# Merging heads while the last pair is divided, sparse scores three steps ahead, and part of the compressed branch on GpSimd

## What is computed

```
for l in range(DEPTH):
    h = modulate(rms_norm(x, norm1_g[l]), sh1, sc1)
    qa, ka, va, qb, kb, vb, ga, gb = split_in_proj(h @ w_in[l])
    ya = window_attention_latent(rope(qa), rope(ka), va, kac, vac, sink_a[l])
    yb = full_attention_latent(rope(qb), rope(kb), vb, kbc, vbc)
    x = x + gt1 * ((sigmoid(ga) * (ya @ w_pa) + sigmoid(gb) * (yb @ w_pb)) @ w_o)
    x = x + gt2 * swiglu(modulate(rms_norm(x, norm2_g[l]), sh2, sc2), ...)
```

```
s = q @ kc + bias;  p_cmp = masked_softmax(s, dist >= 0);  o_cmp = p_cmp @ vc
s = q @ kb + bias;  o_slc = masked_softmax(s, causal) @ vb
s = q @ kw + bias;  o_win = masked_softmax(s, causal) @ vw
y_a = (sum of sigmoid(br_gate) * (o_cmp, o_slc, o_win)) * silu(g_nsa) @ w_proj_a
```

## Time and profile before

| | |
|---|---|
| timed runs, us | 2504.87, 2505.83, 2508.88 (median 2505.83) |
| profiled execution | 2507.7 us, its span 2505.8 us |
| TensorE busy | 2395.6 us, 96%, 13215 matmuls |
| VectorE busy | 1570.5 us, 63%, 2476 instructions |
| ScalarE busy | 1121.6 us, 45%, 1776 instructions |
| GpSimd busy | 146.1 us, 6%, 261 instructions |
| mean granted clock of TensorE | 0.985 of 2.4 GHz |
| weight splits on VectorE (L185) | 288 of 1.22 us |
| mean DMA rate | 107 GB/s |

### The profile page before, as it was taken

The page is one execution under the profiler, slowest core; times in us unless marked ns, Lnnn a source line. Parts: engine busy times, 40 slices in busy tenths (PEclk is TensorE's granted clock), DMA queues, the critical chain, the costliest instruction groups (busy, mean ns, idle before and its releaser), DMA issues.

```text
span 2505.8 us, 34512 instructions
## 1 busy us (share of the span) xinstructions
PE 2395.6 (96%) x13215; PEld 2047.7 (82%) x13215; DVE 1570.5 (63%) x2476; ACT 1121.6 (45%) x1776; POOL 146.1 (6%) x261
## 2 busy tenths in 40 slices
PE   7999999899999999999999998999999999888898
PEld 3888878788888888888778876899999978777677
DVE  4776777788666554454676776644443565487764
ACT  4647777723321121122647775332222355565541
POOL 0200000110000000000100001000000010000010
PEclk8999999999999999999999999999999999999999
DMA  6421111353333333322221113422222333421153
GB/s 278 145 72 45 52 38 45 120 227 125 145 134 118 125 128 135 118 76 84 101 76 52 51 51 128 141 85 95 91 95 91 110 114 139 143 80 61 69 200 110
DMA packets 67961, 268.88 MB, mean 107 GB/s; under 512 B 8432, under 2 KB 8496, under 8 KB 66528
## 3 DMA queue, kind: packets, MB, share of 16 engines
q1 hardware_dynamic: 42336, 162.94, 18.4%
q0 software_dynamic: 25472, 103.82, 11.6%
HBM read 238.42 MB, written 27.26 MB: 106 GB/s over the span
## 4 chain that ended last, share of the span: by engine, by line
PE 80%; DVE 6%; issue 6%; ACT 5%; DMA 2%; POOL 0%; SPq 0%; ACTq 0%; DVEq 0%; POOLq 0%
PE ps L189 22%; PE ps L191 22%; PE ps L190 22%; PE ps L1199 1%; PE ps L1200 1%; PE ps L1201 1%; PE ps L1133 1%; PE ps L1140 1%; DMA ada_raw<-in_ada 1%; DVE inv L1385 1%; PE ps L1182 1%; ACT pr L1263 1%; PE ps L813 1%; DVE maxes L1358 1%; PE ps L1217 1%
## 5 line engine op out<-in xcount | busy, mean ns | idle before, releaser
L189 PE MATMUL ps<-h_hi,w_hi 128*128 128x512 f32 (+2 forms) x2680 | 920.8, 344 | 28.8 <-DVE h_lo L1479 15.1
L191 PE MATMUL ps<-h_hi,w_lo 128*128 128x512 f32 (+2 forms) x2680 | 907.1, 338 | 0.0
L190 PE MATMUL ps<-h_lo,w_hi 128*128 128x512 f32 (+2 forms) x2680 | 906.6, 338 | 0.0
L189 PEld LDWEIGHTS ps<-h_hi,w_hi 128*128 128x128 f32 x2680 | 509.5, 190 | 91.4 <-issue 29.6
L191 PEld LDWEIGHTS ps<-h_hi,w_lo 128*128 128x128 f32 x2680 | 509.1, 190 | 56.9
L190 PEld LDWEIGHTS ps<-h_lo,w_hi 128*128 128x128 f32 x2680 | 508.8, 190 | 55.7 <-issue 2.4
L185 DVE TENSOR_TENSOR w_lo<-w_raw,w_hi 128x1024 fp32r<-128x1024 f32 x288 | 351.9, 1223 | 166.5 <-ACT w_hi L178 166.3
L178 ACT ACTIVATE w_hi<-w_raw 128x1024 fp32r<-128x1024 f32 x288 | 302.6, 1052 | 306.5 <-PE ps L191 292.0
L191 PE MATMUL ps<-q_hi,w_lo 128*128 128x512 f32 x720 | 256.8, 357 | 0.0
L190 PE MATMUL ps<-q_lo,w_hi 128*128 128x512 f32 x720 | 256.5, 356 | 0.0
L189 PE MATMUL ps<-q_hi,w_hi 128*128 128x512 f32 x720 | 256.1, 356 | 0.0
(11 more groups left out here) (358 smaller groups left out, 3058.7 us busy)
## 6 DMA issues: line engine op xcount, KB each, us to landing
w_raw<-in_stream SPq DMA_DIRECT2D x288, 512.0 KB, 3.5
wt<-in_ada_t POOLq DMA_DIRECT2D x72, 512.0 KB, 3.8
ada_raw<-in_ada SPq DMA_DIRECT2D x4, 2048.0 KB, 19.1
x_keep<-x POOLq DMA_DIRECT2D x8, 768.0 KB, 7.1
gates<-th_g POOLq DMA_DIRECT2D x16, 384.0 KB, 2.6
x<-x_keep POOLq DMA_DIRECT2D x2, 3072.0 KB, 12.3
gates<-sg POOLq DMA_DIRECT2D x24, 256.0 KB, 2.3
wt_q<-in_ada_t POOLq DMA_DIRECT2D x8, 512.0 KB, 3.8
```

Of the source, the lines that this page charges most:

```text
L189: nc.tensor.matmul(out_ap, lh, rh, start=start, stop=False)
L190: nc.tensor.matmul(out_ap, lh, rl, start=False, stop=False)
L191: return nc.tensor.matmul(out_ap, ll, rh, start=False, stop=stop)
```

## The change

Four things are changed.

- TensorE's wait for the memsets (`ready.base + 4`) moves from step -8 to `turn(0)`, which is the first to read `maxes` (`spread` is read later, by `sink`).
- `h_hi` of the first pairs (two in layer 0, three in layer 1) is copied by ScalarE inside the attention's last steps (`pair_high`). VectorE's steps end at T; the last pair's `divide` moves into the merge, piece by piece between the first `h_lo`s. TensorE does the first four chunks of unit 0 and of unit 1 in turn, then the rest of 0, then the rest of 1. The wait for `y_taken` comes ahead of unit 1's second half, and the one for `taken` ahead of all.
- In the sparse attention three gate chunks stand ahead of the first scores instead of one, `scores` run three steps ahead and behind the turn (they were two ahead and in front of it), gate chunks three ahead (one before). ScalarE's `gate` is at step 5 of a head (it was step 0 of the next). VectorE's `cmp_shift` is at step 0 (was 1), its weight split at step 4 (was 1), and `cmp_scale` is cut in two: `cmp_sum` stays on VectorE at step 3, and the product with the branch gate and the last product run on GpSimd, as does `prep` from head 2 on. GpSimd has its own order (`pool_own`).
- The semaphores of "nsa", "lru" and "cmp" are taken from the one shared set "second".

```diff
+            y_high, = signals("heads", y_high=CH)
+            early_pair = {T - 1: 0, T + 1: 1} if both else {T - 1: 0, T: 1, T + 1: 2}
...
                     if n == 0:
+                        e.wait_ge(ready.sem, ready.base + 4)
...
                     for q in now:
                         gate_chunk(q)
-                    if t == -PRO:
-                        e.wait_ge(ready.sem, ready.base + 4)
...
+                    if t in early_pair:
+                        if t == T - 1:
+                            e.wait_ge(unit_done, 1 + base + N_GATE)
+                        pair_high(e, early_pair[t])
+            def pair_high(e, c):
+                e.wait_ge(divided.sem, divided.base + parts * (c + 1))
+                nc.scalar.activation(h_hi[:, c, 0:wide], qf[:, c, 0:wide], ACT.Copy).then_inc(y_high.sem, 1)
+            def divide(e, u, piece):
...
-                for t in range(-PRO, T + LAG + 10):
+                for t in range(-PRO, T):
...
-                    for u in range(NU):
+                    for u in range(NU - parts):
                         n = parts * (2 * (u // parts) + 1) + u % parts
                         since = t - (final[n] + LAG + 3 + 2 * (u % parts))
                         if 0 <= since < pieces[n]:
-                            divide(u, since)
...
+                def chunk(n, c):
+                    at, s, cols = 2048 * (n % 2) + 1024 * (c // 4), (base + n) % 3, slice(c * P, c * P + P)
                     if n == 0:
-                        e.wait_ge(done["gated"].sem, done["gated"].base + N_GATE)
-                        e.wait_ge(done["maxed"].sem, done["maxed"].base + done["tiles"])
-                    elif n == 1:
-                        e.wait_ge(done["taken"].sem, done["taken"].base + done["ring"])
-                        e.wait_ge(done["y_taken"].sem, done["y_taken"].base + done["outputs"])
-                    else:
-                        e.wait_ge(gated.sem, gated.base + n - 1)
+                        e.wait_ge(y_low.sem, y_low.base + c + 1)
+                    for s0, size in groups:
+                        mm = three(psf[:, at + s0:at + s0 + size], w_hi[:, s, cols], w_lo[:, s, cols],
+                                   h_hi[:, c, s0:s0 + size], h_lo[:, c, s0:s0 + size], c % 4 == 0, c % 4 == 3)
+                    return mm
+                e.wait_ge(lo_ready, base + 2)
+                e.wait_ge(done["gated"].sem, done["gated"].base + N_GATE)
+                e.wait_ge(done["maxed"].sem, done["maxed"].base + done["tiles"])
+                e.wait_ge(done["taken"].sem, done["taken"].base + done["ring"])
+                for c in range(4):
+                    chunk(0, c)
+                    chunk(1, c)
+                for c in range(4, 8):
+                    mm = chunk(0, c)
+                mm.then_inc(unit_done, 1)
+                e.wait_ge(done["y_taken"].sem, done["y_taken"].base + done["outputs"])
+                for c in range(4, 8):
+                    mm = chunk(1, c)
+                mm.then_inc(unit_done, 1)
+                for n in range(2, CH):
+                    e.wait_ge(lo_ready, base + n + 1)
+                    e.wait_ge(gated.sem, gated.base + n - 1)
                     for c in range(CH):
-                        if n == 0:
-                            e.wait_ge(y_low.sem, y_low.base + c + 1)
-                        at, s, cols = 2048 * (n % 2) + 1024 * (c // 4), u % 3, slice(c * P, c * P + P)
-                        for s0, size in groups:
-                            mm = three(psf[:, at + s0:at + s0 + size], w_hi[:, s, cols], w_lo[:, s, cols],
-                                       h_hi[:, c, s0:s0 + size], h_lo[:, c, s0:s0 + size], c % 4 == 0, c % 4 == 3)
+                        mm = chunk(n, c)
                     mm.then_inc(unit_done, 1)
             def act(e):
-                e.wait_ge(unit_done, 1 + base)
-                for c in range(CH):
-                    e.wait_ge(done["divided"].sem, done["divided"].base + parts * (c + 1))
-                    nc.scalar.activation(h_hi[:, c, 0:w], qf[:, c, 0:w], ACT.Copy).then_inc(y_high.sem, 1)
+                for c in range(done["pairs_high"], CH):
+                    done["pair_high"](e, c)
...
+                last = parts * (CH - 1)
                 for c in range(CH):
                     e.wait_ge(y_high.sem, y_high.base + c + 1)
                     nc.vector.tensor_tensor(h_lo[:, c, 0:w], qf[:, c, 0:w], h_hi[:, c, 0:w].bitcast(F32), ALU.subtract).then_inc(y_low.sem, 1)
+                    if c < 2:
+                        done["divide"](e, last, 2 * c)
+                        done["divide"](e, last, 2 * c + 1)
+                    if c == 2 and parts == 2:
+                        done["divide"](e, last + 1, 0)
+                        done["divide"](e, last + 1, 1)
...
-                gate_chunk(0)
+                for q in range(3):
+                    gate_chunk(q)
                 e.wait_ge(cmp["biased"].sem, cmp["biased"].base + 2)
                 e.wait_ge(cmp["gated"].sem, cmp["gated"].base + 12)
                 scores(0)
                 scores(1)
+                scores(2)
                 for n in range(M):
-                    if n + 2 < M:
-                        scores(n + 2)
                     if n % 8 == 0:
                         cmp_scores(n // 8)
                     turn(n)
+                    if n + 3 < M:
+                        scores(n + 3)
                     if n % 8 == 4:
                         cmp_turn(n // 8)
                     if n % 4 == 1 and n >= 4:
                         values(n // 4 - 1)
-                    if n + 1 < M:
-                        gate_chunk(n + 1)
+                    if n + 3 < M:
+                        gate_chunk(n + 3)
...
-                    if n % 8 == 0 and n:
-                        gate(n // 8 - 1)
+                    if n % 8 == 5:
+                        gate(n // 8)
...
-                def cmp_scale(hd):
-                    pair, g = hd // 2, hd % 2
-                    at = 4 * g + pair
+                def cmp_sum(hd):
                     e.wait_ge(c_exp.sem, c_exp.base + hd + 1)
                     dve_own.link(e, nc.vector.tensor_reduce(cmp_n[:, 1, :], cmp_s[:, :, :], AX_X, ALU.add))
-                    dve_own.link(e, nc.vector.reciprocal(cmp_n[:, 2, :], cmp_n[:, 1, :]))
-                    dve_own.link(e, nc.vector.tensor_tensor(cmp_n[:, 3, :], br_cols[:, :, at:at + 1].rearrange("p r a -> p (r a)"),
-                                                            cmp_n[:, 2, :], ALU.mult))
-                    dve_own.link(e, nc.vector.scalar_tensor_tensor(cmp_s[:, :, :], bias_of(hd), -NEG / 2, cmp_s[:, :, :],
-                                                                   ALU.is_lt, ALU.mult))
-                    nc.vector.tensor_tensor(cmp_s[:, :, :], cmp_s[:, :, :], bc(cmp_n[:, 3, :]), ALU.mult).then_inc(c_scaled.sem, 1)
+                    nc.vector.reciprocal(cmp_n[:, 2, :], cmp_n[:, 1, :])
+                    nc.vector.scalar_tensor_tensor(cmp_s[:, :, :], bias_of(hd), -NEG / 2, cmp_s[:, :, :], ALU.is_lt,
+                                                   ALU.mult).then_inc(c_summed.sem, 1)
...
-                    if n % 8 == 1:
+                    if n % 8 == 0:
+                        cmp_shift(hd)
+                    if n % 8 == 4:
                         split_lo(e, base + hd + 2)
-                        cmp_shift(hd)
-                    if n % 8 == 2 and 1 <= hd and hd + 1 < H:
-                        prep(hd + 1)
                     if n % 8 == 3:
-                        cmp_scale(hd)
+                        cmp_sum(hd)
...
+                def prep(hd):
+                    pair, g = hd // 2, hd % 2
+                    e.wait_ge(a_ready.sem, a_ready.base + 2 * hd + 1)
+                    nc.gpsimd.tensor_tensor(qb[half[g], hd % 2, :], qf2[half[g], pair, :], qa[half[g], hd % 2, :].bitcast(F32),
+                                            ALU.subtract).then_inc(b_ready.sem, 1)
+                    e.wait_ge(b_ready.sem, b_ready.base + hd + 1)
+                def cmp_scale(hd):
+                    pair, g = hd // 2, hd % 2
+                    at = 4 * g + pair
+                    e.wait_ge(c_summed.sem, c_summed.base + hd + 1)
+                    pool_own.link(e, nc.gpsimd.tensor_tensor(cmp_n[:, 3, :], br_cols[:, :, at:at + 1].rearrange("p r a -> p (r a)"),
+                                                             cmp_n[:, 2, :], ALU.mult))
+                    nc.gpsimd.tensor_tensor(cmp_s[:, :, :], cmp_s[:, :, :], bc(cmp_n[:, 3, :]), ALU.mult).then_inc(c_scaled.sem, 1)
+                    e.wait_ge(c_scaled.sem, c_scaled.base + hd + 1)
                 e.wait_ge(cmp["spilled"].sem, cmp["spilled"].base + 64)
                 for hd in range(2):
                     e.dma_start(bias[:, hd, :], bias_in[4 * (hd % 2) + hd // 2]).then_inc(here[hd % 2].sem, 16)
                 for i in range(G):
                     hd = i + 2
```

(3 more changed lines are left out.)

58 lines of the change are left out of this document (28 added, 30 removed).

## The result

The changed kernel takes 2487.86 us (median of 6 runs, 2484.92 to 2491.22) against 2506.41 us for the kernel before in the same comparison (6 runs). The ratio is 0.9922 with a 95% interval of 0.9909 to 0.9935, so 16 to 23 us are gone. The forecast was 2485.7 us with a range of 2475 to 2497. The profiled execution has a span of 2487.1 us.

The account below looks back on a forecast made before the run. TensorE works nearly without a pause, so the gain is how much earlier it gets operands at its few pauses. 2.2 + 1.4 + 4.8 + 1.7 + 10.0 = 20.1 us off 2505.8 gave 2485.7 us, range 2475 to 2497.

Parts of the forecast that it names:

- Part 1: Attention entries: the wait for `ready` moved to `turn(0)` gains 2.2 us in layer 1, 1.4 in layer 0.
- Part 2: Layer 0's merge: TensorE alone 6.9 us ahead, VectorE's rounds take some back at the last `q_lo`; 4.8 us left.
- Part 3: Layer 1's merge: same order, but a late weight transfer limits the gain; 1.7 us, bounds 0.4 and 4.2.
- Part 4: Sparse attention: shorter chains to waited turns, gate chunks in the first pause, some clock; 10.0 us, bounds 4 and 16.
- chain count: Sparse attention, VectorE's steps between turns: net 0.7 us for three heads, 0.5 for three, -0.2 for the last.
- GpSimd's room: Sparse attention: 2.4 us before TensorE wants GpSimd's result, 1.0 us taken for both products, so hidden.
- (a): Rival, 17%: VectorE takes back more than counted in merges and sparse attention; 11 us gained, 2495 us.
- (b): Rival, 10%: the clock stays full in the sparse part and in layer 1's merge; 2474 us.
- (c): Rival, 12%: GpSimd's and VectorE's pieces hold each other up in the sparse attention; 8 us lost, 2493 us.
- (d): Rival, 6%, slower: GpSimd's start-up and semaphores delay `cmp_turn` in eight heads; 2518 us at 6.5 us per head.
- (e): Rival, 5%: last pair's copies and sums are the true wait; merges and late heads give nothing; 2503 us.

Follow-up runs that it names:

- m1: m1_merge_only: the kernel before with only the merge part of the diff (early `h_hi`, division between the `h_lo`, units in turn); 2502.11 us, ratio 0.9976.
- m2_side_back: The changed kernel with GpSimd's side work (`prep` and both products) back on VectorE at its former steps; 2492.88 us, ratio 0.9953 to the kernel before.
- n4_units_one_by_one: The changed kernel with the first two units of both merges done one after the other instead of in turn; 2489.4 us, ratio 0.9926 to the kernel before.
- p3_gates_one_ahead: The changed kernel with gate chunks one step ahead again and ScalarE's `gate` back at step 0 of the next head; 2496.43 us.
- m4_pool_later: The changed kernel with five memsets on GpSimd ahead of its two products, which start some 2.8 us later; 2501.5 us.
- n2_split_in_gap: The changed kernel with the sparse attention's weight split on VectorE moved from step 4 to step 2; 2484.89 us, ratio 0.9911 to the kernel before.
- p1_x_and_split: The changed kernel with the merges' load of `x` cut in two and the weight split in step 2; 2478.5 us, ratio 0.9893 to the kernel before.
- p2_and_y_in_two: The changed kernel with `x` load cut in two, weight split in step 2, and VectorE's `y_lo` moved to step 4; 2479.23 us.

## Why the prediction was right, and where not

The sum was 20.1 us; the median moved by 18.5 and the ratio says 16 to 23. That it is so close is in part luck: in the profile after, layer 0's entry and layer 1's merge gave nothing of the 3.1 us forecast for them, while the sparse attention gave 1.4 us more than its term and unchanged code 0.8. Term by term:

| term | forecast | shown |
|---|---|---|
| layer 0, entry of the attention | 1.4 (1.0 to 1.4) | 1.4 to 1.7 in six traces, 0.0 to 0.3 in six |
| layer 0, merge | 4.8 (2.6 to 6.9) | 5.2 |
| layer 1, entry of the attention | 2.2 (1.7 to 3.4) | 1.8 at the entry, 1.4 by the end of the attention; 1.6 to 1.8 against m1, where the clock fell later on in both |
| layer 1, merge | 1.7 (0.4 to 4.2) | 0.0 in the profile after, -2.4 to 3.0 elsewhere |
| sparse attention | 10.0 (4 to 16) | 11.4 (11.2 to 13.0 in five traces) |

**Part 1.** In layer 1 the mechanism came as written: no wait for `spread`, and one of 4.52 us for `qa`. The chunk ahead of it ran 4.1 us earlier, the next one 1.76 us. The 0.5 us on top, for less work in the slow stretch, did not show: 1.8 us was all. In layer 0 the wait went and 1.6 us was there at once. In six of twelve profiles it was taken back within 5 us. No run moves this wait back alone, so the term is read from the traces. The windows of TensorE behind the entry, in the changed kernel and in m2_side_back:

```profile
171.80:176.00 4.20, 4.12 (x16) 0.59 0.78 226
```

```profile
171.00:176.00 5.00, 4.58 (x27) 1.00 0.66 229
```

The same 1.77 us wait for `qa` stands ahead of both. The step that failed is "at the least 1.0": I let the clock fall in layer 1 only, behind the long pause, and gave the short one none. The two outcomes go together. In the six traces that kept the gain here, the clock fell at the wait of 1.65 us in layer 1's attention; in the six that lost it, it fell there in one (n4_units_one_by_one). The code at both places is the same in all twelve. Why the outcomes alternate is open.

**Part 2.** The chain of steps was right in nearly every number: waits of 0.74, 0.80, 1.04 and 0.81 us where "under 1" and "about 1" stood, TensorE 9.3 - 2.5 = 6.8 us ahead where 6.9 was forecast, and VectorE's rounds taking a part back at the last `q_lo`. That wait was 1.36 us instead of 1.9. The term that was mis-sized is VectorE's own round: the 8.44 us of the earlier trace rows were also TensorE's time for a unit (8.45), and with TensorE ahead the rounds took 8.39 us. Over seven rounds VectorE caught up 0.4 us, which is the whole difference between 4.8 and 5.2.

**Part 3.** The first half was right: the wait for `h_lo` 1 is 2.62 us (forecast 2.7). The clock, 0.80 in that stretch, fell only in part, and the next wait was 0.35 us where up to 1.8 stood, so TensorE was 3.8 us ahead. What failed is the last step, "between 0.4 and the 3.0 of full clock I take the middle". I had seen the late weight unit and the load of `x` beside it, and then assumed that both move with the merge. The load isn't a fixed length, its landing scatters by 3 us, and the stage ends where it ends. The fall of the clock behind the late gate product, 1.6 us here, was in no term. The lower bound of 0.4 was wrong; it should have been some 2.5 us below nothing.

**Part 4.** The size was nearly right, two of its terms were not. The step given to GpSimd was taken as a small saving (0.2 us each for L2225 and L2229, hidden `prep`): alone it was worth 5.4 us (m2_side_back). And the gate chunks' lead was taken as 1.6 us of filled pauses: with ScalarE's `gate` it was worth 8.4 us in its trace, half of it clock (p3_gates_one_ahead), since it also brings the bias loads ahead. The prediction named GpSimd's queue only for the products; the bias loads that stand in it behind a wait were missing, and with them 8.6 us of ScalarE's waiting in the profile before. The parts are not additive, 5.4 + 8.4 is more than 11.4. The chain count itself holds roughly. It gave 0.5 us a head without a `y` and 0.7 with one. From one compressed turn to the next 18.86 us became 18.2 without a `y` (18.6 where the clock fell in it), and 21.1 to 21.4 became 20.2 to 20.7 with one. By place, 3.5 us were there at the first compressed turn (forecast 2.7 for head 0 and the chunks' share of 1.6), 2.4 in the next four heads, and 5.5 in the last three, of which about 3 are clock (2.3 was taken).

**GpSimd's room** was the prediction's clearest error in a part that cost nothing: it took 2.4 us from the rows of a head with a `y`, where there is plenty. Without one there was 0.3 us left, as m4_pool_later made plain.

**The rivals.** (a), 2495 us, is 7 us off where the forecast is 2 off, and its parts are wrong: layer 0's merge gave 5.2 us where it has 2.6, and the sparse attention 11.4 where it has 4.3. (b), a full clock everywhere, did not come: 2474 was not reached, though the granted clock of the late heads rose from 0.89 to 0.96 over the same steps. (c) two engines that stop each other: m2_side_back, with no GpSimd beside VectorE, was slower by 5 us, not faster. But its mechanism exists. In the changed kernel it fell on GpSimd: a `prep` that starts 0.17 us ahead of the end of a `scale` on VectorE takes 1.30 us, one that starts 0.31 us ahead of it 1.44, and each ends 1.13 us behind it, while the `scale` keeps its 0.55 us. In n2_split_in_gap, p1_x_and_split and p2_and_y_in_two it fell on VectorE, the six `scale` of 0.91 to 1.05 us. In m4_pool_later three weight splits, which read two tiles in SBUF, started beside GpSimd's product and took 1.38 us, and the five beside its memsets alone took 1.22. The rule of the Trainium skill (SBUF — State Buffer, Who interferes with whom) agrees with this for the splits, except that a split lost 0.16 us while the two ran beside each other for 0.3, so it was not held for the whole of that time; whether `scale` runs in a two-port mode no trace tells. GpSimd's product at 2221.74 ran beside a VectorE product that reads PSUM, and that one took 0.68 us as before the change. What (c) had wrong for this kernel is the size and the side: the waits were GpSimd's, and they were covered. (d) is what m4_pool_later does. (e) fell with m1_merge_only.

## What to carry to other kernels

Compare two traces by the n-th matmul of the same line at stage boundaries, and judge an edit in its own stage: here one stage repeated to 0.1 us while unchanged code moved by 4 us, and n4_units_one_by_one, which cost 4.0 us in its stage, was invisible in the total. Then part a stage's gain into waits and clock by its busy time: the waits belong mostly to the edit, the clock partly to the chance of that one execution. Before pricing a reordering, list every DMA that is issued behind a moved wait, with who uses it: the bias load behind a gate was worth more than the matmuls that the edit spoke of. And what a stage gains can be kept only until its next DMA: with the load of `x` brought forward into idle time layer 1's merge kept 3.8 to 3.9 us in all three traces that have it, where it had kept -2.4 to 3.0.

## What the runs showed of the hardware

A wait of TensorE of 1.65 to 1.77 us is followed by a fall of the granted clock in some executions of the same code and not in others (0.59 against 1.00, 0.84 against 1.00 in the windows above). By the table the fall cost 1.1 to 1.7 us in layer 0's attention and about 1 us in layer 1's. A 3 MB load took 12.5 to 15.5 us to land when issued at the same place of the program. GpSimd's elementwise product of 128x128 elements took 0.40 us where VectorE took 0.29, and the difference of 64x512 elements 1.3 to 1.45 us where VectorE took 0.69. VectorE's `scale` of 128x512 elements took 0.91 to 1.05 us beside that difference on GpSimd, and 0.55 us otherwise.
